# A product-key expert layer on one core: the late up-units in 512-column products, with a copy and a sum behind them and their low halves on GpSimd

## The reference, cut to what matters

```
best_v, best_pos = lax.top_k(cand_v, PEER_TOPK)
idx = jnp.take_along_axis(cand_i, best_pos, axis=-1)
gate = jax.nn.softmax(best_v, axis=-1)
...
u = u_tab[ix]
act = jax.nn.gelu(jnp.einsum('chkd,cd->chk', u, hx))
vv = v_tab[ix]
return jnp.einsum('chk,chkd->cd', gx * act, vv)
```

## Time and profile before

| | |
|---|---|
| device time, median of 3 runs (lowest, highest) | 1877.83 us (1876.46, 1878.59) |
| span of the profiled execution | 1874.2 us |
| outside the span, against the median | 3.6 us |
| PE busy in the span | 1824.1 us, 97% |
| DVE busy | 1305.0 us, 70% |
| ACT busy | 922.9 us, 49% |
| POOL busy | 116.3 us, 6% |

### The profile page before, as it was taken

One profiled execution on the slowest core, in us unless ns is written; L12 is line 12 of the kernel. 1 busy time (PEld: TensorE's weight loads), 2 busy tenths in 40 slices (PEclk: granted clock), 3 DMA queues, 4 the chain that ended last, 5 costly groups with the idle time before them and its releaser, 6 DMA issues.

```text
span 1874.2 us, 30697 instructions
## 1 busy us (share of the span) xinstructions
PE 1824.1 (97%) x12639; PEld 1677.6 (90%) x12639; DVE 1305.0 (70%) x2098; ACT 922.9 (49%) x1238; POOL 116.3 (6%) x75
## 2 busy tenths in 40 slices
PE   7999899999999999999999999999999999989998
PEld 7999899999999999988888888888888889878887
DVE  5567875999788888755555557887577445757744
ACT  6447635444344343444444445766455343546533
POOL 0000002670000000000000000030000000100000
PEclk9999999999999999999999999997999999989999
DMA  6444345454444443465555553421155456625543
GB/s 236 162 159 161 132 180 204 168 188 170 153 155 147 146 158 137 160 232 193 189 200 186 195 197 124 148 83 64 65 183 179 178 200 221 175 96 206 186 169 145
DMA packets 44757, 310.66 MB, mean 166 GB/s; under 512 B 5182, under 2 KB 5694, under 8 KB 8160
## 3 DMA queue, kind: packets, MB, share of 16 engines
q1 hardware_dynamic: 42592, 303.58, 44.9%
q0 software_dynamic: 1472, 4.86, 1.4%
q10 hardware_dynamic: 576, 0.55, 0.1%
HBM read 306.84 MB, written 2.13 MB: 165 GB/s over the span
## 4 chain that ended last, share of the span: by engine, by line
PE 69%; DVE 12%; ACT 2%; issue 1%; POOL 0%; ACTq 0%; DVEq 0%
PE bank L347 20%; PE bank L1706 18%; PE bank L3034 9%; PE bank L358 6%; PE bank L362 3%; PE bank L1677 3%; PE bank L3293 2%; DVE s_arena L1846 1%; DVE s_ring_lo L310 1%; PE bank L446 1%; PE bank L2659 1%; DVE s_arena L1843 1%; DVE s_arena L1889 1%; DVE s_arena L2121 1%; PE bank L2597 1%
## 5 line engine op out<-in xcount | busy, mean ns | idle before, releaser
L310 DVE TENSOR_TENSOR s_ring_lo<-s_ring,s_w_hi 128x2048 fp32r<-128x2048 f32 x227 | 519.7, 2290 | 173.1 <-ACT s_w_hi L304 168.6
L304 ACT ACTIVATE s_w_hi<-s_ring 128x2048 fp32r<-128x2048 f32 x244 | 465.8, 1909 | 132.1 <-PE bank L347 42.3
L347 PE MATMUL bank<-s_h_r,s_w_hi 128*128 128x256 f32 x3072 | 405.2, 285 | 0.3 <-DVE s_arena L3522 0.3
L347 PEld LDWEIGHTS bank<-s_h_r,s_w_hi 128*128 128x128 f32 x3072 | 381.7, 192 | 4.8 <-issue 3.6
L1706 PE MATMUL bank<-s_w_hi,s_h_r 128*128 128x512 f32 x1008 | 238.8, 389 | 0.3 <-issue 0.3
L1706 PEld LDWEIGHTS bank<-s_w_hi,s_h_r 128*128 128x128 f32 x1008 | 189.2, 188 | 39.6 <-issue 0.4
L347 PE MATMUL bank<-s_h_r,s_ring_lo 128*128 128x256 f32 x1536 | 215.7, 283 | 1.4 <-DVE s_ring_lo L310 1.4
L347 PEld LDWEIGHTS bank<-s_h_r,s_ring_lo 128*128 128x128 f32 x1536 | 198.1, 192 | 1.8 <-DVE s_ring_lo L310 1.8
L1806 ACT ACTIVATE s_h_r<-s_arena 128x512 fp32r (+1 forms) x64 | 40.4, 632 | 184.6 <-PE bank L1706 184.6
L3006 DVE TENSOR_TENSOR s_ring_lo<-s_ring,s_spare_r 128x2048 fp32r<-128x2048 f32 x32 | 73.1, 2291 | 78.6 <-ACT s_spare_r L2992 78.6
L1706 PE MATMUL bank<-s_ring_lo,s_h_r 128*128 128x512 f32 x504 | 124.5, 389 | 0.0
(11 more groups left out here) (464 smaller groups left out, 2501.3 us busy)
## 6 DMA issues: line engine op xcount, KB each, us to landing
s_ring<-weights SPq DMA_DIRECT2D x282, 1024.0 KB, 4.8
s_arena<-bias_by_distance POOLq DMA_DIRECT2D x12, 384.0 KB, 7.9
s_arena<-mem SPq DMA_DIRECT2D x1, 1024.0 KB, 5.7
s_x<-x SPq DMA_DIRECT2D x1, 1024.0 KB, 13.4
x_away<-s_x SPq DMA_DIRECT2D x1, 1024.0 KB, 7.9
s_arena<-sub_keys SPq DMA_DIRECT2D x1, 1024.0 KB, 11.0
s_arena<-x_away SPq DMA_DIRECT2D x1, 1024.0 KB, 8.4
out<-s_x SPq DMA_DIRECT2D x2, 512.0 KB, 2.6
```

Of the source, the lines that this page charges most:

```text
L304: act.activation(k.w_hi[:, u % 2, :], k.ring[:, u % RING, :], ACT.Copy).then_inc(k.hi_ready, 1)
L310: dve.tensor_tensor(k.ring_lo[:, u % RING, :], k.ring[:, u % RING, :], plain(k.w_hi[:, u % 2, :]), ALU.subtract).then_inc(k.lo_ready, 1)
L347: last = pe.matmul(out[:, nb * S:(nb + 1) * S], w[:, c, nb * P:(nb + 1) * P], h[:, c, :], start=(n == 0 and c == 0), stop=(n == 2 and c == 7))
```

## The change

Units 20 to 63 go through a new function, `unit_T_banks`. It multiplies each high weight block by low and high activations in one product of 512 columns (`h_swapped`), and the low blocks by the high activations in 256 columns: 32 products in place of 48. Each half `nb` of the unit has a bank of its own (ps[0], ps[1]), whose left 256 columns hold high-by-low and whose right 256 the two other products. ScalarE copies the left half to SBUF (`cross`), VectorE adds the right half to it into ps[2 + j % 2] (`join`), and Gelu and combine work there. The groups have four banks in place of six. GpSimd makes the low halves of units 22 to 64, VectorE none in this stage, and `heat(g+1)` moves to the front of VectorE's turn. Two pairs of semaphores become counts of one each, and `joined`, a tile of 256 columns, shares its place with `gdn_small`.

```diff
+def unit_T_banks(k, pe, u, h_hi, h_swapped, banks, half_done, free):
+    hi, lo = unit_parts(k, u)
+    split_ready(k, pe, u, 0)
+    for nb in range(2):
+        free(nb)
+        for c in range(8):
+            pe.matmul(banks[nb][:, :], hi[:, c, nb * P:(nb + 1) * P], h_swapped[:, :, c, :], start=(c == 0), stop=False)
+        if nb == 0:
+            split_ready(k, pe, u, 2)
+        for c in range(8):
+            last = pe.matmul(banks[nb][:, S:2 * S], lo[:, c, nb * P:(nb + 1) * P], h_hi[:, c, :],
+                             start=False, stop=(c == 7))
+        if nb == 0:
+            last.then_inc(half_done, 1)
+    last.then_inc(k.unit_done, 1)
...
-    bank = [ps[2 + g % 6] for g in range(GROUPS)]
+    bank = [ps[4 + g % 4] for g in range(GROUPS)]
+    across = k.joined[:, :]
+    h_swapped = k.h_r[:, 0:2]
...
-            elif j - 2 < EARLY_R:
+            elif j < EARLY_R:
                 pe.wait_ge(gelu_out, j - 1)
-            else:
-                pe.wait_ge(combined, j - 1 - EARLY_R)
-            unit_T_split(k, pe, split_unit(j), *h_pair, ps[j % 2])
+            if j < EARLY_R:
+                unit_T_split(k, pe, split_unit(j), *h_pair, ps[j % 2])
+                return
+            def free(nb):
+                if j == EARLY_R:
+                    pe.wait_ge(gelu_out, EARLY_R - 1 + nb)
+                else:
+                    pe.wait_ge(summed, 2 * (j - 1 - EARLY_R) + nb + 1)
+            unit_T_banks(k, pe, split_unit(j), k.hT_hi, h_swapped, ps[0:2], half_done, free)
...
-            if g >= 6:
-                pe.wait_ge(spread_out, g - 5)
+            if g >= 4:
+                pe.wait_ge(spread_out, g - 3)
...
+            act.wait_ge(summed, 2 * (j - EARLY_R + 1))
+            act.activation(ps[2 + j % 2][:, :], ps[2 + j % 2][:, :], ACT.Gelu_apprx_tanh).then_inc(gelu_out, 1)
...
+        def cross(j):
+            for nb in range(2):
+                if nb == 0:
+                    act.wait_ge(half_done, j - EARLY_R + 1)
+                else:
+                    act.wait_ge(k.unit_done, F + j + 1)
+                if j > EARLY_R or nb:
+                    act.wait_ge(summed, 2 * (j - EARLY_R) + nb)
+                act.activation(across, ps[nb][:, 0:S], ACT.Copy).then_inc(crossed, 1)
...
             if g >= 1:
                 copy(g - 1)
+            if g in up_at:
+                cross(up_at[g])
...
-        for u in range(Q + 2, F + POOL_R):
+        for u in (*range(Q + 2, F + POOL_R), *range(F + EARLY_R + 2, F + PAIRS + 1)):
...
+        def join(j):
+            for nb in range(2):
+                dve.wait_ge(crossed, 2 * (j - EARLY_R) + nb + 1)
+                dve.tensor_tensor(ps[2 + j % 2][:, nb * S:(nb + 1) * S], ps[nb][:, S:2 * S], across,
+                                  ALU.add).then_inc(summed, 1)
...
         for g in range(GROUPS + 1):
+            if g + 1 < GROUPS:
+                heat(g + 1)
             if g in up_at and up_at[g] > EARLY_R:
                 combine(up_at[g] - 1, max(g - 1, 0))
-                split_lo(k, dve, split_unit(up_at[g] + 1))
             if g >= 1:
                 multiply(g - 1)
-            if g + 1 < GROUPS:
-                heat(g + 1)
+            if g in up_at:
+                join(up_at[g])
...
+            if d == 0:
+                dve.wait_ge(k.lo_ready, F + PAIRS + 1 - k.whole_units)
             split_lo(k, dve, split_unit(PAIRS + d + 1), turn=i * 4)
...
-        k.gdn_small = sb("gdn_small", [P, 7, 4, GDN_H])
+        k.joined = sb("joined", [P, S])
+        k.gdn_small = k.joined[:, 0:7 * 4 * GDN_H].rearrange("p (a b c) -> p a b c", a=7, b=4)
```

More of the change, by code:

```diff
@@ L1595, in peer @@
     x_back = carve(k, 0, TT, D)
-    names = ("keys_here", "q_out", "score_mm", "score_out", "shift_ready", "exp_ready",
-             "chosen_ready", "chosen_turned", "slots_ready", "h_split", "gelu_out", "hot_ready", "spread_mm",
+    names = ("keys_here", "q_out", "score_mm", "score_out", "dve_prepared", "act_prepared", "half_done", "crossed", "summed",
+             "chosen_ready", "chosen_turned", "slots_ready", "gelu_out", "hot_ready", "spread_mm",
              "multiplied", "spread_out", "combined", "weighted_round", "weighted_ready", "bank_done",
[L1599 to L1602, removed]
+             "query_scaled")
+    (keys_here, q_out, score_mm, score_out, dve_prepared, act_prepared, half_done, crossed, summed, chosen_ready, chosen_turned,
+     slots_ready, gelu_out, hot_ready, spread_mm, multiplied, spread_out, combined, weighted_round,
+     weighted_ready, bank_done, query_scaled) = (ctx_sem(k, n) for n in names)
     own = k.steps
@@ L1610, in peer @@
     up_at = up_turns()
-    bank = [ps[2 + g % 6] for g in range(GROUPS)]
+    bank = [ps[4 + g % 4] for g in range(GROUPS)]
+    H_SPLIT, SHIFTED = 1, 2
+    QUERY_SPREAD, EXPS = 1, 2
+    across = k.joined[:, :]
+    h_swapped = k.h_r[:, 0:2]
     def present(g):
@@ L1650, in score @@
             if h == 1:
-                pe.wait_ge(query_spread, 1)
+                pe.wait_ge(act_prepared, QUERY_SPREAD)
             if h >= 2:
@@ L1725, in tensor @@
         score(PEER_H - 1)
-        pe.wait_ge(h_split, 1)
+        pe.wait_ge(dve_prepared, H_SPLIT)
         for j in range(EARLY_R):
@@ L1765, in scalar @@
                 act.wait_ge(k.turned, 4 * k.norms + 1)
-                act.activation(begin.spread, ps[3][:, 0:S], ACT.Copy).then_inc(query_spread, 1)
+                act.activation(begin.spread, ps[3][:, 0:S], ACT.Copy).then_inc(act_prepared, 1)
             if h == 2:
@@ L1771, in gelu @@
         def gelu(j):
-            act.wait_ge(k.unit_done, F + j + 1)
-            out = flat(k.G[:, 2 * j:2 * j + 2, :]) if j < EARLY_R else ps[j % 2][:, :]
-            act.activation(out, ps[j % 2][:, :], ACT.Gelu_apprx_tanh).then_inc(gelu_out, 1)
+            if j < EARLY_R:
+                act.wait_ge(k.unit_done, F + j + 1)
+                act.activation(flat(k.G[:, 2 * j:2 * j + 2, :]), ps[j % 2][:, :], ACT.Gelu_apprx_tanh)\
+                   .then_inc(gelu_out, 1)
+                return
+            act.wait_ge(summed, 2 * (j - EARLY_R + 1))
+            act.activation(ps[2 + j % 2][:, :], ps[2 + j % 2][:, :], ACT.Gelu_apprx_tanh).then_inc(gelu_out, 1)
         def copy(g):
@@ L1785, in copy @@
                .then_inc(spread_out, 1)
+        def cross(j):
[3 more added lines that the diff above has]
+                else:
+                    act.wait_ge(k.unit_done, F + j + 1)
+                if j > EARLY_R or nb:
+                    act.wait_ge(summed, 2 * (j - EARLY_R) + nb)
+                act.activation(across, ps[nb][:, 0:S], ACT.Copy).then_inc(crossed, 1)
         for j in range(EARLY_R):
             if j == EARLY_R - 4:
-                act.wait_ge(shift_ready, 1)
-                act.activation(shifted, shifted, ACT.Exp).then_inc(exp_ready, 1)
+                act.wait_ge(dve_prepared, SHIFTED)
+                act.activation(shifted, shifted, ACT.Exp).then_inc(act_prepared, 1)
             gelu(j)
@@ L1869, in vector @@
         factor()
-        dve.wait_ge(query_spread, 1)
+        dve.wait_ge(act_prepared, QUERY_SPREAD)
         for n in range(KC):
@@ L1879, in vector @@
                 dve.wait_ge(k.x_saved, 16)
-                dve.tensor_tensor(k.x_r[:, :], flat(scaled), plain(flat(k.hT_hi)), ALU.subtract).then_inc(h_split, 1)
+                dve.tensor_tensor(k.x_r[:, :], flat(scaled), plain(flat(k.hT_hi)), ALU.subtract).then_inc(dve_prepared, 1)
             dve.wait_ge(score_out, h + 1)
@@ L1895, in vector @@
         first = top[:, :, :, 0:1].to_broadcast([P, TT, PEER_H, TOPK])
-        dve.tensor_tensor(shifted, top, first, ALU.subtract).then_inc(shift_ready, 1)
+        dve.tensor_tensor(shifted, top, first, ALU.subtract).then_inc(dve_prepared, 1)
         for n, (amount, op) in enumerate(((4, ALU.logical_shift_right), (2, ALU.logical_shift_right),
@@ L1939, in vector @@
                 own.settle(dve)
-        dve.wait_ge(exp_ready, 1)
+        dve.wait_ge(act_prepared, EXPS)
         own.up(dve.tensor_reduce(total, shifted, AX.X, ALU.add))
@@ L1979, in combine @@
             dve.wait_ge(gelu_out, j + 1)
-            act, at = halves(ps[j % 2][:, :]), k.G[:, 2 * j:2 * j + 2, :]
+            act, at = halves(ps[2 + j % 2][:, :]), k.G[:, 2 * j:2 * j + 2, :]
             if t:
```

## The result

The changed kernel takes 1948.82 us (median; 1944.38 to 1949.63) against 1877.14 for the kernel before on the same chip: ratio 1.0376, 95% interval 1.0361 to 1.039, 72 us slower. Forecast were 1981 us and a range of 1940 to 2030. Way and cause came out as forecast; the loss is 72 us rather than 103, 30% smaller.

What follows compares the result with a forecast made beforehand. TensorE was taken to bound the kernel, busy for all but 0.3 of the late stage's 308.3 us. 100 for 20 pairs, 1.7 at the end and about 1 for the last unit gave +103: 1981 us, range 1940 to 2030.

Steps and rivals of the forecast that it cites:

- partly held: Rival: VectorE gets more than one piece of `heat` through between two subtractions; +30 to +80, 1908 to 1958 us; chance 0.03.
- main case: Late stage: all of `heat` stands while GpSimd subtracts, 19.2 us a pair in place of 14.18; chance 0.83.
- The ring: Seven-step walk from one GpSimd subtraction to the same point of the next pair: 19.20 us against 14.18, no product in it.
- the three waits of TensorE: 5.5 us of gaps a pair: first low product (GpSimd late), second group (tables late), each unit's first bank (sum late).
- Step 2: VectorE finishes the rest of `heat` after GpSimd's two subtractions, at most one of five pieces having slipped in: 1.39 us.
- Steps 4 and 5: Step 4: copy, sum, copy, sum, 1.76 us. Step 5: next `heat` 1.77 with its wait, `multiply` 0.41, `copy` 0.34: 2.52 us.
- step 7: Handovers between engines not contained in the other steps of the walk: 0.25 us a pair.
- That every beat is alike: 20 pairs of late units, after three undisturbed units, each 5.0 us longer: +100 us.
- The end: After the last product: copy, `round_up`, subtraction and handovers take 2.0 us in place of 0.3: +1.7 us.
- Only L1961 stands: Rival: L1958 doesn't stand, GpSimd's ring of 14.6 us a pair is longest; +10, 1888 us; chance 0.07.
- TensorE stays the bound: Rival: no `heat` stands on the ring, which comes below 13.7 us; 8.6 us less, 1869 us; chance 0.04.
- The clock falls: Addition: TensorE's new gaps halve its clock; +40, 2021 us if for one pair in four; chance 0.15 within the 0.83.

Runs made afterwards that it cites:

- psum_early: tables_from_psum with ScalarE doing gelu and split_hi right behind a unit's crosses, not a unit later behind a group's copy: 1870.82 us, ratio 0.997.
- narrow_psum: Kernel before, with GpSimd making the late low halves and the numbers the tables read copied to PSUM, five group banks: 1876.48 us, ratio 1.0003.
- first_half_psum: Changed kernel with only the tables' tensor_scalar (L2007) reading its numbers from PSUM, the tensor_tensor left on SBUF: 1884.69 us, ratio 1.0043.
- quarters: Changed kernel with each of GpSimd's late subtractions cut into four of 512 columns: 1898.42 us, ratio 1.0113.
- tables_from_psum: Changed kernel with the numbers that both halves of the tables read copied to PSUM, three group banks in place of four: 1886.92 us, ratio 1.005.
- early: Changed kernel, tables in SBUF, with ScalarE doing gelu and split_hi right behind a unit's crosses, not a unit later: 1971.69 us, ratio 1.05.

## Why the prediction was right, and where it was off

The mechanism came about as forecast, and the measured time lies in the range. It also lies in that of the rival "partly held" (1908 to 1958), so the number alone does not tell the two apart; the beats do, and sixteen of twenty are of the main case. Two terms were mis-sized, and that both together stayed inside the range is in part luck.

**What bounds the stage, and the gain.** Right. TensorE was the bound, and what the wide products can give is small: 0.46 us a pair were worked out, psum_early shows 0.32. The first half behind a group takes 2.88 us rather than the 2.80 of the earlier trace rows. One reading was off: unit 20 starts right behind the transposes at 472.2 us, and 475.0 is its second half. The stage before is thus 311.1 us; the sum went by beats, so nothing hung on it.

**Which operations stand.** Right, and shown by narrow_psum, first_half_psum and quarters. L1958, which no row showed beside GpSimd, was judged by its pace; it stands, though no run shows that the pace is the reason. `join`, `multiply` and `combine` kept theirs (join 0.43, as taken). The section "SBUF: two separate sides" of the page "SBUF — State Buffer" of the Trainium skill says that the hold is for the whole instruction; quarters agrees, with at most 1342 ns of a `tensor_scalar` behind pieces of 1342 ns in the mean.

**The beat.** The ring is the one that was walked, with the three waits of TensorE where they were put, but two terms were mis-sized.
- *Step 2, the rest of `heat`* was taken at 1.39 us, with at most one of five pieces through. GpSimd ends at 644.50 and `combine` starts at 645.36, so the rest was 0.9: two pieces had passed by 640.03, a third, which stood from 639.96, ended with GpSimd's second subtraction, and only the last piece of L2007 and L2010 were still to come. The other 0.3 us is spread over the walk. Steps 4 and 5 took 0.2 less (consecutive instructions of one engine overlap by some 0.1 us: a copy of 0.34 starts at 646.72, the next at 646.95), and the handovers of step 7 took 0.07 rather than 0.25. GpSimd's two subtractions took 9.36 rather than 9.26. Together 18.37 rather than 19.20, over 16 beats 13 us.
- *That every beat is alike.* Four of the twenty were of 15.1 us. Timeline of one:

```profile
544.26 3.25 PE L360 MATMUL bank<-s_h_r,s_w_hi 128*128 128x512 f32 x8 [1.27 <-DVE bank L2042]
...
549.80 4.61 POOL L1883 TENSOR_TENSOR s_ring_lo<-s_ring,s_w_hi 128x2048 fp32r<-128x2048 f32 x1 [8.97 <-ACT s_w_hi L304]
...
551.66 0.38 ACT L1832 ACTIVATE s_joined<-bank 128x256 f32<-128x256 f32 x1 [1.20 <-PE bank L364]
...
552.56 2.70 DVE L2007 TENSOR_SCALAR s_hT<-s_consts,s_slots 128x128 f32<-128x128 f32 x4
...
555.02 5.29 POOL L1883 TENSOR_TENSOR s_ring_lo<-s_ring,s_w_hi 128x2048 fp32r<-128x2048 f32 x1 [0.61 <-ACT s_w_hi L304]
555.19 0.68 DVE L2010 TENSOR_TENSOR s_hT<-s_consts,s_slots 128x512 f32<-128x512 f32 x1
```

Here a cross waited for TensorE's product, so `gelu` and `split_hi` came late, GpSimd's second subtraction was not ready when the first ended at 554.41, and the whole of `heat` passed between the two (GpSimd's second took 5.29 us, as if it had stood for L2010 in its turn).

The cross was late because TensorE was: the eight wide products at 544.26 took 3.25 us where they take 2.09 at full clock. Six of the twenty beats had a granted clock of 0.91 in the mean. All four short beats are among the six that follow one of these; none follows a beat at full clock. In the other two the second subtraction came 0.56 us behind the first rather than 0.61 or 0.62, and VectorE's fourth `tensor_scalar` was caught again. This is read from one trace, not tested.

Over four beats this is 4.1 us each, 16 us. From 494.63 to 849.83 GpSimd's rows give 16 beats of 18.4 and 4 of 15.1: 355.2 us where 20 x 14.18 = 283.6 stood, +71.6; the forecast was +100. The prediction had this mechanism among its rivals ("partly held") with a chance of 0.03, as something for all beats rather than for one in five. The range had room for it by its doubt of slipping pieces (-35).

**The end** was put at +1.7: TensorE was idle for 1.76 us before the first down-product (860.24) where it had 0.27. Right. What is left to the 75.1 us of the stage, 2 us, lies outside the twenty beats. Outside it the profiled execution was 1.9 us shorter, which is within what such executions differ; it wasn't followed up.

**The rivals.** *Only L1961 stands* and *TensorE stays the bound* did not come about, but the ring of 14.6 us behind the first is what tables_from_psum ran at (14.72), and the second is psum_early. *The clock falls* came about mildly: 0.97 over the stage. The +40 that it was given did not come: the six beats with a clock of 0.91 took 18.34 to 18.50 us, the full-length ones at full clock 18.36 to 18.57. No product is in the ring, so slower products only shortened TensorE's waits.

## What to carry to other kernels

Before work goes from VectorE to GpSimd, list what VectorE does in the meantime by where its operands lie: with two inputs in SBUF, or with its one tensor input and its output there as L1958 has, it stood here until GpSimd's instruction ended, although by their busy times both engines had room. Such an operation can be freed by one operand in PSUM (60 ns for each `tensor_scalar` here, and all of the 29 us came back), or the hold shortened by cutting GpSimd's instruction. And when one resource is relieved, walk the ring that leads back to it with the order of each engine's list: here the products had 0.3 us a pair to give, 7 in all, and one change in the order of ScalarE's list moved the time by 16 us down where the tables could not stand, and by 23 up where they could and TensorE came back from its waits at a lower clock. A low clock cost nothing in the changed kernel, whose ring holds no product, and by the estimate above 28 us in early, whose ring does.

## What the hardware showed beyond that

- An operation that stands is booked as busy on VectorE, from its turn on. The stage's VectorE load rose from 262 to 318 us while its work fell.
- The granted clock fell below full inside a stage in which TensorE was busy for most of the time. Stretches of the changed kernel:

```profile
540.00:545.00 5.00, 2.88 (x20) 2.44 (x19) 3.63 (x9) 1.07 (x3) 0.83 (x1) 0.98 0.54 210
545.00:550.00 5.00, 5.00 (x20) 4.22 (x20) 4.64 (x15) 2.95 (x4) 0.20 (x1) 0.67 0.00 0
550.00:555.00 5.00, 4.90 (x31) 4.10 (x31) 3.31 (x6) 3.25 (x5) 4.41 (x1) 1.00 0.45 154
```

  Behind 2.88 busy of 5 us the mean was 0.67, a mix of 1.2 and 2.4 GHz, and full again in the next stretch. In early it was 0.90 over the whole stage, in psum_early 1.00.
